# First half of both feed forwards in two quarters, its down projection by seven half-block products of a Strassen scheme

## What is computed

```python
def sq_relu_mlp(x, w_up, w_down):
    h = jnp.square(jax.nn.relu(x @ w_up))
    return h @ w_down
...
x = layer_norm(DN_ALPHA * x + sq_relu_mlp(x, w_up[layer], w_down[layer]),
               ln_g[layer, 1], ln_b[layer, 1])
```

## Time and profile before

| what | value |
|---|---|
| median of 3 runs | 1208.98 us (1207.71 to 1209.41) |
| the profiled execution, first to last instruction | 1208.6 us |
| TensorE busy | 1161.6 us, 96% of the span, 5888 matmuls |
| VectorE busy | 635.5 us, 53% |
| ScalarE busy | 493.0 us, 41% |
| GpSimd busy | 129.4 us, 11% |
| weights read from memory | 64 loads each of 512 KB of w_up and of w_down |

### The profile page before, as it was taken

The page is one execution under the profiler, slowest core; times in us unless marked ns, Lnnn a source line. Parts: engine busy times, 40 slices in busy tenths (PEclk is TensorE's granted clock), DMA queues, the critical chain, the costliest instruction groups (busy, mean ns, idle before and its releaser), DMA issues.

```text
span 1208.6 us, 16807 instructions
## 1 busy us (share of the span) xinstructions
PE 1161.6 (96%) x5888; PEld 977.0 (81%) x5888; DVE 635.5 (53%) x1056; ACT 493.0 (41%) x860; POOL 129.4 (11%) x156
## 2 busy tenths in 40 slices
PE   6999999999999999999989999889999999999997
PEld 6777779888888888789868888779888888888886
DVE  4477766644332444345577777766544323445226
ACT  4345635634212343224755656445543212334120
POOL 2300035200000000023300101026200000000000
PEclk9999999999999999999999999899999999999999
DMA  7422132333333333332212122112332333333332
GB/s 221 131 70 70 53 99 74 90 89 102 105 87 104 88 104 87 105 90 76 80 53 71 53 56 66 35 53 76 99 104 87 105 101 90 87 94 96 105 105 87
DMA packets 185590, 107.22 MB, mean 89 GB/s; under 512 B 4482, under 2 KB 180162, under 8 KB 185540
## 3 DMA queue, kind: packets, MB, share of 16 engines
q1 hardware_dynamic: 180112, 99.36, 28.2%
q10 hardware_dynamic: 5428, 7.18, 1.9%
HBM read 104.43 MB, written 2.10 MB: 88 GB/s over the span
## 4 chain that ended last, share of the span: by engine, by line
PE 73%; DVE 5%; ACT 5%; issue 4%; POOL 1%; DMA 0%; DVEq 0%; ACTq 0%; POOLq 0%; SPq 0%
PE proj L499 58%; PE pv L499 3%; PE sc L499 2%; PE proj L808 2%; PE sc L808 2%; PE pv L808 2%; PE tr L808 2%; PE tr L547 1%; DVE w_lo L1415 1%; ACT w_hi L1028 1%; ACT x L1184 1%; ACT x_hi L1186 1%; POOL total L1995 0%; DVE neg_max L1470 0%; DVE split_lo L1415 0%
## 5 line engine op out<-in xcount | busy, mean ns | idle before, releaser
L1415 DVE TENSOR_TENSOR w_lo<-w_raw,w_hi 128x1024 fp32r<-128x1024 f32 x173 | 219.7, 1271 | 172.9 <-ACT w_hi L1028 124.8
L499 PE MATMUL proj<-x_hi,w_hi 128*128 128x512 f32 (+1 forms) x768 | 298.9, 390 | 2.6 <-ACT x_hi L1186 1.2
L499 PE MATMUL proj<-x_hi,w_lo 128*128 128x512 f32 (+1 forms) x768 | 294.2, 384 | 0.0
L499 PE MATMUL proj<-x_lo,w_hi 128*128 128x512 f32 (+1 forms) x768 | 288.7, 383 | 0.0
L1028 ACT CAST w_hi<-w_raw 128x1024 fp32r<-128x1024 f32 x160 | 166.9, 1044 | 169.2 <-PE proj L499 167.1
L499 PEld LDWEIGHTS proj<-x_hi,w_hi 128*128 128x128 f32 x768 | 145.1, 189 | 29.6 <-ACT x_hi L1186 2.8
L499 PEld LDWEIGHTS proj<-x_hi,w_lo 128*128 128x128 f32 x768 | 145.0, 189 | 28.8
L499 PEld LDWEIGHTS proj<-x_lo,w_hi 128*128 128x128 f32 x768 | 142.2, 188 | 25.4
L499 PE MATMUL proj<-h_hi,w_hi 128*128 128x512 f32 (+1 forms) x384 | 146.4, 381 | 2.5 <-DVE w_lo L1415 2.5
L499 PE MATMUL proj<-h_hi,w_lo 128*128 128x512 f32 (+1 forms) x384 | 146.0, 380 | 0.0
L499 PE MATMUL proj<-h_lo,w_hi 128*128 128x512 f32 (+1 forms) x384 | 146.0, 380 | 0.0
(11 more groups left out here) (325 smaller groups left out, 1812.8 us busy)
## 6 DMA issues: line engine op xcount, KB each, us to landing
w_raw<-in_w_up SPq DMA_DIRECT2D x64, 512.0 KB, 4.0
w_raw<-in_w_down SPq DMA_DIRECT2D x64, 512.0 KB, 3.6
w_raw<-in_w_o SPq DMA_DIRECT2D x16, 512.0 KB, 3.6
w_raw<-in_a_w_in SPq DMA_DIRECT2D x14, 512.0 KB, 3.8
w_raw<-in_kv_w SPq DMA_DIRECT2D x12, 512.0 KB, 3.8
w_raw<-in_mem_w_kv SPq DMA_DIRECT2D x8, 512.0 KB, 5.4
w_raw<-in_b_w_q SPq DMA_DIRECT2D x8, 512.0 KB, 3.6
x_nat<-in_x ACTq DMA_DIRECT2D x2, 1024.0 KB, 11.6
```

The costliest lines, as they stand in the source:

```text
L499: last = pe.matmul(target, lhs, rhs, start=start and n == 0, stop=stop and n == len(terms) - 1)
L1415: return dve.tensor_tensor(target, whole, hi.bitcast(F32), ALU.subtract)
```

## The change

The first half of each feed forward becomes two quarters of eight up units and four pairs. A pair is two output tiles. For a pair the eight hidden tiles of the quarter are taken as four even and odd neighbours, the 512 tokens as two halves of 256, and the product of 2x2 blocks (output tile by hidden tile, times hidden tile by token half) is formed with seven block products in place of eight, in Winograd's form of Strassen's scheme. Each of the seven (an item, `ITEMS`) is four 128x128 stationary blocks by 256 tokens, three matmuls each.

- GpSimd adds four sums of weight blocks for a pair (`weight_sums`), each 128x512; the other three items take raw weights.
- ScalarE casts and VectorE takes the rest of each item, 128x512, in a ring of eight places (`item_cast`, `item_rest`); four of the places lie in w_hi and w_lo.
- After an up unit VectorE makes the square and, for each even and odd neighbour, four sums and differences of 128x256 (`form_squares`); ScalarE casts and VectorE takes the rest of 512 numbers per partition after the even tile and of 1280 after the odd one (`form_cast`, `form_rest`).
- The items' results lie in four half banks. VectorE works them into x32 with eight instructions for each pair, and ScalarE copies the first item's result away (`down_pair`, `copy_first`). Two of the half banks are used twice in a pair without being cleared.
- The weights of a pair are 1 MB in one of two places: pair_raw for even pairs, w_raw, the place of the up units, for odd ones (`load_pair`).
- The loops over up and down units of that half are written out on TensorE, ScalarE and VectorE. Unit and bank numbers behind it move; nothing else does.

The core of the diff, without the second half's lines (only shifted there), the addresses and the renumbering. ScalarE's list for a quarter is: for each of eight up units the cast of the next unit, the cast of the odd form behind an even unit, relu, and the cast of the even form; ahead of the last relu the casts of items 0 to 3, behind it those of items 4 to 6, the last form, and then the items of the pairs in order, with `copy_first` of the pair before behind each item 0; last the next up unit.

```diff
+    QT, QP = KT, KT // 2
+    H_T1, H_B11, H_B21, H_B22, H_T2, H_T3, H_T4 = range(7)
+    S_1, S_2, S_3, S_4 = range(4)
+    ITEMS = [("A11", H_B11), (S_2, H_T2), (S_1, H_T1), (S_3, H_T3), ("A12", H_B21), (S_4, H_B22), ("A22", H_T4)]
+    N_ITEMS = len(ITEMS)
+    RING = 8
+    E_U, E_12, E_2, E_M5, E_M7, E_11, E_12B, E_21, EVICTS = *range(1, 9), 8
...
+        pair_raw = put("pair_raw", [P, 2, KT, P], F32, top + 56 * K1)
+        w_sum = put("w_sum", [P, 4, QP, P], F32, L0)
+        cross = put("cross", [P, HT], F32, L0 + 8 * K1)
+        first_product = put("first_product", [P, HT], F32, L0 + 9 * K1)
+        h_form = put("h_form", [P, 8, HT], F32, low)
+        relu_q = put("relu_q", [P, 2, T], F32, MV0)
...
+            def load_pair(layer, q, p):
+                number, b, _ = quarter(layer, q)
+                n = QP * number + p
+                if p % 2 == 0 and n % (2 * QP) == 0:
+                    sp.wait_ge(w_used, (B_UP[0][0] + 2, B_UP[1][0] + 4)[layer])
+                elif p == 1:
+                    sp.wait_ge(w_split, b + QT)
+                else:
+                    sp.wait_ge(item_split, item(n - 1, 0))
+                for c in range(2):
+                    sp.dma_start(raw_pair(n)[:, c], cols(w_down[layer], (2 * p + c) * P, q * D)).then_inc(pair_landed[n % 2], 16)
...
+            def cross_products(n, i, tiles=range(QP)):
+                _, h = ITEMS[i]
+                bank = cross_banks()[(0, 3, 1, 2, 0, 1, 2)[i]]
+                pe.wait_ge(item_split, item(n, i) + 1)
+                if tiles[0] == 0:
+                    if i == 4:
+                        pe.wait_ge(first_copied, n + 1)
+                    else:
+                        wait(pe, evicted, (E_11, E_U, E_12B, E_21, None, E_M5, E_M7)[i] + EVICTS * (n - (i < 4)))
+                hi, lo = ring(n, i)
+                for k in tiles:
+                    if n % QP == 0:
+                        pe.wait_ge(form_ready, 2 * (n + k) + (1 if h in (H_T1, H_B11) else 2))
+                    for m, (w, x) in enumerate(((hi[:, k], hb_hi[:, k, h]), (hi[:, k], hb_lo[:, k, h]), (lo[:, k], hb_hi[:, k, h]))):
+                        last = pe.matmul(bank, w, x, start=i < 4 and k == 0 and m == 0, stop=k == QP - 1 and m == 2,
+                                         skip_group_check=True)
+                return last
+            def down_pair(n):
+                if n % QP:
+                    for i in range(N_ITEMS):
+                        cross_products(n, i).then_inc(item_used, 1)
+                    return
+                cross_products(n, 0).then_inc(item_used, 1)
+                cross_products(n, 2)
+                early = range(QP - 1)
+                for i in (1, 3):
+                    cross_products(n, i, early)
+                cross_products(n, 1, range(QP - 1, QP)).then_inc(item_used, 2)
+                cross_products(n, 3, range(QP - 1, QP)).then_inc(item_used, 1)
+                for i in range(4, N_ITEMS):
+                    cross_products(n, i).then_inc(item_used, 1)
...
+            def item_cast(n, i):
+                if i == 0:
+                    act.wait_ge(pair_landed[n % 2], 32 * (n // 2 + 1))
+                form, at = ITEMS[i][0], N_ITEMS * (n % QP) + i
+                if form in range(4):
+                    act.wait_ge(sum_ready, 4 * n + form + 1)
+                if at >= RING:
+                    act.wait_ge(item_used, item(n, i) - RING + 1)
+                elif at >= RING // 2:
+                    act.wait_ge(w_used, B_UP[n // (2 * QP)][0] + n // QP % 2 * QT + QT - 2 + at // 2 - 1)
+                elif n:
+                    act.wait_ge(item_used, item(n, at) - RING // 2 + 1)
+                act.copy(ring(n, i)[0], item_source(n, i)).then_inc(item_hi, 1)
+            def copy_first(n):
+                act.wait_ge(item_used, item(n, 0) + 1)
+                wait(act, evicted, EVICTS * (n - 1) + E_U)
+                act.copy(first_product[:, :], cross_banks()[0]).then_inc(first_copied, 1)
...
+            def form_squares(layer, q, t):
+                number, _, g = quarter(layer, q)
+                count, made = 2 * layer * FT + q * QT + t, 4 * (QP * number + t // 2)
+                dve.wait_ge(proj_free[g % 2 ^ t % 2], (g + t) // 2 + 1)
+                wide = relu_q[:, t % 2, :].rearrange("p (h t) -> p h t", h=2)
+                at = 3 if t % 2 else 1
+                dve.tensor_tensor(h_form[:, at:at + 2], wide, wide, ALU.mult).then_inc(relu_sq, 1)
+                dve.wait_ge(relu_sq, count + 1)
+                if t % 2 == 0:
+                    dve.tensor_tensor(h_form[:, 0], h_form[:, 1], h_form[:, 2], ALU.subtract).then_inc(form_made, 1)
+                    return
+                dve.wait_ge(form_made, made + 1)
+                dve.tensor_tensor(h_form[:, 5], h_form[:, 4], h_form[:, 0], ALU.add).then_inc(form_made, 1)
+                dve.tensor_tensor(h_form[:, 6], h_form[:, 4], h_form[:, 2], ALU.subtract).then_inc(form_made, 1)
+                dve.wait_ge(form_made, made + 2)
+                dve.tensor_tensor(h_form[:, 7], h_form[:, 5], h_form[:, 3], ALU.subtract).then_inc(form_made, 1)
...
+            def down_pair(n):
+                a, scale, first = 2 * (n % QP), (1.0 if n // QP % 2 else ALPHA), EVICTS * n
+                x11, x12 = x32[:, a, 0:HT], x32[:, a, HT:T]
+                x21, x22 = x32[:, a + 1, 0:HT], x32[:, a + 1, HT:T]
+                both = x32[:, a + 1, :].rearrange("p (h t) -> p h t", h=2)
+                twice = cross[:, :].rearrange("p (a t) -> p a t", a=1).broadcast_to([P, 2, HT])
+                one, two, three, six = cross_banks()
+                def done(i):
+                    dve.wait_ge(item_used, item(n, i) + 1)
+                def ahead(i):
+                    m, at = n + (i + 1) // N_ITEMS + 1, (i + 1) % N_ITEMS
+                    if m // QP == n // QP:
+                        item_rest(m, at)
+                done(0)
+                ahead(0)
+                done(1)
+                dve.wait_ge(first_copied, n + 1)
+                dve.tensor_tensor(cross[:, :], first_product[:, :], six, ALU.subtract).then_inc(evicted, 1)
+                ahead(1)
+                dve.wait_ge(evicted, first + E_U)
+                dve.scalar_tensor_tensor(out=x12, in0=x12, scalar=scale, in1=cross[:, :], op0=ALU.mult, op1=ALU.add).then_inc(evicted, 1)
+                dve.scalar_tensor_tensor(out=both, in0=both, scalar=scale, in1=twice, op0=ALU.mult, op1=ALU.subtract).then_inc(evicted, 1)
+                ahead(2)
+                done(2)
+                dve.wait_ge(evicted, first + E_2)
+                dve.tensor_tensor(x22, x22, two, ALU.subtract).then_inc(evicted, 1)
+                ahead(3)
+                done(3)
+                dve.wait_ge(evicted, first + E_M5)
+                dve.tensor_tensor(x22, x22, three, ALU.subtract).then_inc(evicted, 1)
+                ahead(4)
+                done(4)
+                dve.scalar_tensor_tensor(out=x11, in0=x11, scalar=scale, in1=one, op0=ALU.mult, op1=ALU.add).then_inc(evicted, 1)
+                ahead(5)
+                done(5)
+                dve.tensor_tensor(x12, x12, two, ALU.add).then_inc(evicted, 1)
+                ahead(6)
+                done(6)
+                dve.tensor_tensor(x21, x21, three, ALU.subtract).then_inc(evicted, 1)
...
+                for q in range(2):
+                    number, b, g = quarter(layer, q)
+                    first = QP * number
+                    for t in range(QT):
+                        if t < QT - 1 and (q or t > 2):
+                            prepare(Pos(b + t + 1))
+                        if t % 2:
+                            form_rest(first + t // 2, False)
+                        elif t:
+                            form_rest(first + t // 2 - 1, True)
+                        if t == QT - 1:
+                            for i in range(4):
+                                item_rest(first, i)
+                        form_squares(layer, q, t)
+                    for i in range(4, 6):
+                        item_rest(first, i)
+                    form_rest(first + QP - 1, True)
+                    item_rest(first, 6)
+                    item_rest(first + 1, 0)
+                    for p in range(QP):
+                        down_pair(first + p)
+                        if p == QP - 2:
+                            prepare(Pos(b + QT))
...
+            def weight_sums(n):
+                even, odd = ([raw_pair(n)[:, c, parity::2, :] for c in range(2)] for parity in range(2))
+                pool.wait_ge(pair_landed[n % 2], 32 * (n // 2 + 1))
+                for form, one, other in ((S_1, even[1], odd[1]), (S_2, even[0], w_sum[:, S_1]), (S_3, even[0], even[1]),
+                                         (S_4, odd[0], w_sum[:, S_2])):
+                    wait(pool, item_split, item(n - 1, [own[0] for own in ITEMS].index(form)) + 1)
+                    if form in (S_2, S_4):
```

(14 more changed lines are left out.)

466 lines of the change are left out of this document (260 added, 206 removed).

## The result

The changed kernel takes 1257.6 us (median of 4 runs, 1255.8 to 1260.6), the kernel before 1209.1: ratio 1.0402, 95% interval 1.0389 to 1.0415. It is 48.5 us slower. The forecast of 1238 had the sign and the places of the waits; its sum of +28.8 us was 20 us short. The profiled span is 1254.1 us against 1208.6, and the 45.5 us between them lie in the changed stretches: layer 0's second half starts at 415.63 us, before at 391.56 (+24.1), layer 1's at 1069.86, before at 1024.36 (+45.5).

A forecast was written before the change was run, and what follows sets the result against it. TensorE was taken to bound the kernel (96% busy). Per quarter -3.2 + 0.4 + 2.4 + 0.7 + 3.3 + 2.8 + 0.8 = +7.2 us, +28.8 for four, so 1208.98 became 1238 us; range 1208 to 1258.

The forecast's parts named there:

- gain of the items: Down part of a quarter: 336 matmuls of 256 columns replace 192 of 512, saving 3.2 us per quarter.
- (1): TensorE waits for the forms of the quarter's last odd tile, without GpSimd's sums: 0.4 us per quarter.
- (2): First pair, before item 5: VectorE's queue delays the bank's eviction to 10.0-10.1 us after U (last up matmul's end); 2.4 us.
- (3): Pairs after the first, without GpSimd's sums: no wait, with 1 us in hand at each eviction.
- (4): Quarter's end: the next up unit's late load puts its rest ahead of the last pair's evictions; 0.7 us.
- (5): At the last form: GpSimd's second-pair sums take turns with VectorE's form work; 3.3 us per quarter (2.7 to 4.0).
- (6): In the second pair: eight sums for the third and fourth pairs delay VectorE's evictions; 2.8 us per quarter (0 to 4).
- (7): In the up units: the first pair's sums delay square, forms and next rest; 0.8 us per quarter (0 to 2.5).
- B: Rival: the SBUF port does not matter, sums fall into VectorE's gaps; 1210 us (1206.6 to 1216), chance 0.14.
- A: Rival: waits lower TensorE's clock to half, with (5) to (7) at their upper ends; 1258 to 1263 us, chance 0.14.
- C: Rival: faster, no port wait and item 5's eviction 1.2 us sooner, waits under the gain; 1204 us, chance 0.07.
- D: Rival: each pair's item 0 waits for the pair before, 1 us for each of 12 later pairs; 1250 us, no separate chance.

The follow-up runs named there:

- 5b: kernel 1 (no weight sums) with the next up unit's rest moved behind the last pair's evictions on VectorE: 1216.0 us, ratio 1.0055.
- kernel 1: Changed kernel without GpSimd's weight sums: one number written for each, raw blocks used instead: 1222.8 us, ratio 1.0119.
- 11: Changed kernel without the sums of each quarter's second pair, the first pair's sums left in place: 1243.4 us, ratio 1.0271.
- kernel 10: Changed kernel without the sums of each quarter's third and fourth pair: 1247.8 us, ratio 1.0325.
- kernel 3: Changed kernel without only the sums of each quarter's first pair: 1241.2 us, ratio 1.0269.
- Kernels 4: Changed kernel, complete, with VectorE's first-pair evictions up to item 2's bank moved ahead of the rests for later items: 1276.2 us, ratio 1.0542.
- 5: kernel 1 with first-pair evictions ahead of later rests, and the next up unit's rest behind the last pair's evictions: 1219.9 us, ratio 1.0088.
- kernel 6: Changed kernel, complete, with the first pair's weights loaded earlier and its four sums spread one by one over up units: 1260.3 us, ratio 1.0414.
- kernel 7: Changed kernel with unused filler matmuls on TensorE ahead of the last up unit and the last form's items: 1261.6 us, ratio 1.0423.
- kernel 2: Changed kernel with each GpSimd sum replaced by a memset about as long, which writes SBUF and reads nothing: 1225.3 us, ratio 1.0127.

## Why the prediction was right in kind and short in size

The steps, per quarter, against what the kernels show. The rows of the sums come from leaving each group out alone; together the three give 40.4 us, but all sums at once give 34.8, since one wait partly hides the next. Waits are counted here from the end of the slot of the matmul before, as the forecast does, 0.16 us more than the rows show.

| step | forecast | measured | from |
|---|---|---|---|
| gain of the items | -3.2 | -3.2 | 5b, quarters with the clock up: -0.08 is 0.65 + 2.34 + 2 x 0.07 - 3.2, to 0.02 |
| first distance after a wait | 0 | 0.07, three times a quarter | 1 |
| (1) last odd form | 0.4 | 0.65 | 1 |
| (2) wait before item 5 | 2.4, until U + 10.0 to 10.1 | 2.34, until U + 10.25 | 1 |
| (3) later pairs | 0 | 0 | 1 |
| (4) end of the quarter | 0.7 | 1.86 | 1, gone in 5b |
| (5) sums at the last form | 3.3 | 3.5 | 11 |
| (6) sums of pairs 3 and 4 | 2.8 | 2.4 | 10 |
| (7) sums in the up units | 0.8 | 4.1 | 3 |

**The gain** was priced rightly. In the changed kernel 143 distances without a wait, from 295.04 to 312.26 us on TensorE's timeline, are 0.120 us each but for the first (0.19), as the earlier trace rows gave. After a real wait the first distance is 0.19 us in place of 0.12; that is all a restart costs.

**The queue of VectorE** (steps 1 and 2) came out to within 0.3 us, from the distances of the earlier trace rows alone. The forecast said that no order of ScalarE or GpSimd changes it. Kernels 4 and 5 changed VectorE's own order, and even then the wait came back one item later.

**Step (4)** had the right cause, as 5b shows, and 1.2 us too little: four quarters of it 4.6 us. In kernel 1's first quarter the load is issued 0.44 us after pair 3's first matmul, where I had put it at that matmul, and ScalarE can start on it 4.26 us later, where I had taken the 3.6 of a down tile. That is 1.1 of the 1.2.

**Step (5)** came out near its middle in part by luck. With undisturbed up units, as in kernel 3, the last form comes at U + 9.34, near the end that strict turns gave (9.5), and in kernel 6 at U + 10.1. In the changed kernel it comes at U + 7.3, 8.4, 10.7 and 8.3 in the four quarters. In the three where it comes early the last up unit takes 7.1 to 8.5 us in place of 5.44, and one or two of the sums have passed when the forms come; in the third quarter all three meet them. So what step (7) had too low made step (5) cheaper.

**Step (7) is the step that failed.** I saw which work meets the first pair's sums, the square, the forms and the next rest, and wrote 2.5 us as its upper end. But then I took 0.8 because the load "may land in the easier unit". It landed in the odd unit in the quarter shown above. The upper end was low as well: four sums against four VectorE instructions by turns cost 4.2 us there, since every VectorE instruction of 256 columns waits for a whole sum. 3.3 us a quarter more than forecast are 13.2 us of the 20 that were missing. Nearly as much, 12.4 us, was missing without any sums (next paragraph), and the overlap of the three groups of sums (5.6 us) goes against both.

**Without sums** I had +1.2 us, and 13.6 were measured; kernel 1's profiled execution has +10.3. Of the 9.1 us between the forecast and that execution, step (4) is 4.6, steps (1) and (2) 0.8, the first distance after each of twelve waits 0.9, and two stretches of 3.4 us at the lower clock 3.0; these add up to 9.3. That execution is 2.1 us under the median of its kernel; what the other executions lose is in no trace.

**The range.** The measured 1257.6 lies 0.4 us inside the range's upper end of 1258, and that is luck. By the ends that steps (5) to (7) state (2.7 to 4.0, 0 to 4, 0 to 2.5 us, against the 6.9 taken) the time could be 1221 to 1252, not 1219 to 1256; the -6.9 of the forecast's working is all three at nothing, which is B. The upper 6 us of the range come from no term; they were left for a part of A.

**The rivals.** B (1210) and C (1204) are out: the first by kernel 1 against the changed kernel, the second because even without a single sum, and with (4) mended, the time is 1216.0. Seven products do not beat eight in this kernel by any order tried, since (1) and (2) take 3.1 us with their restarts and the gain is 3.2. D is out: no later pair waits at its start in kernel 1. A (1258 to 1263) gave nearly the measured time, and its clock is there: in the changed stretches seven intervals at the lower level (the expectation of kernel 7 counted six), 30.7 us in all, with TensorE busy 28.3 us in them, where before has none. At half speed that is at most 14.2 us. How much of it counts is settled in part. In 5b, where nothing else is late, 3.4 us of it cost 1.5 us. In front of a wait that VectorE sets it is mostly swallowed: 2.9 us slower gave 0.34 us later (kernel 10). Between the last form and item 5 it costs nothing. The changed kernel's third quarter has the lower clock there, its fourth has not (timeline):

```profile
935.36 0.36 PE L931 MATMUL sc<-hb_hi,w_hi 128*128 128x256 f32 x1 [0.48 <-DVE ring_lo L1579]
...
1033.15 0.36 PE L931 MATMUL sc<-hb_hi,w_hi 128*128 128x256 f32 x1 [2.19 <-DVE ring_lo L1579]
```

TensorE waits 0.48 us in the one and 2.19 in the other, and item 5 starts 4.56 to 4.57 us after the first matmul with the last form in both, as in kernel 1. Kernel 7 was made to tell the price of the whole and did not. A asked for the port at its upper ends and for a clock that adds to it. Measured are, in the changed kernel, (5) and (6) near their middle, (7) far over its end, and a clock that in part hides behind the port.

## What to carry to other kernels

Two engines that exclude each other by whole instructions should be costed as one queue, and the price is not the length of the short instruction but of the other engine's: a VectorE operation of 0.42 us beside sums of 1.28 costs 1.4 to 1.5. If the place of such work isn't tied down, take the upper end: spreading, holding and reordering here moved waits of 2 to 8 us from one item to another and won 8.6 of 48.5 us at best. And weigh a saving of multiplications against the distance of the smaller matmuls and the waits for new operands: an eighth fewer products was 7% fewer microseconds, and two such waits were as large.

## What was not expected of the hardware

- Turns are strict with the shortest instructions too: three form sums in a row went 1.40, 1.51, 1.51 us for 0.42 (the forecast had left open that they pass as a group).
- The clock fell within a wait of only 2.55 us in the changed kernel (0.85 in the window 256 to 260, then 0.50), and in kernel 10 it stayed up after a wait of 2.35 us at the same instructions. The forecast's rival had thought of 4 us.
- GpSimd instructions that only write, nearly as long and at the same places, leave VectorE's at 0.42 and 0.69 us (kernel 2).
